# Second attention: values multiplied for two heads in one visit, turned probabilities kept in eight tiles

## The reference

```python
q = (rmsnorm_2(q_lat, q_norm_g[l]) @ w_uq[l]).reshape(B, S, H, QK_NOPE + QK_ROPE)
q_rope = rotary(q[..., QK_NOPE:], positions)
kv = (rmsnorm_2(kv_lat, kv_norm_g[l]) @ w_ukv[l]).reshape(B, S, H, QK_NOPE + V_HEAD)
y_mla = causal_block_attention(q, k, v)          # H = 16 heads, V_HEAD = 64, 128-query blocks
merged = (jax.nn.sigmoid(g_rnn) * (y_rnn @ w_proj_rnn[l])
          + jax.nn.sigmoid(g_mla) * (y_mla @ w_proj_mla[l]))
x = x + gate1 * (merged @ w_out[l])
```

## Time and profile before

| | us |
|---|---|
| median of three runs | 1893.08 |
| lowest and highest | 1892.84, 1893.96 |
| the profiled execution | 1891.63 |
| its span | 1889.8 |
| PE busy | 1854.6 |
| DVE, ACT, POOL busy | 1055.6, 754.4, 279.5 |

### The profile page before, as it was taken

How to read it: one execution, slowest core, us unless ns; L and a number is a source line. 1 busy time by engine, 2 the same in 40 slices (tenths; PEclk the granted TensorE clock), 3 DMA queues, 4 the chain that set the end, 5 groups by cost and what they waited for, 6 DMA issues and landing times.

```text
span 1889.8 us, 21234 instructions
## 1 busy us (share of the span) xinstructions
PE 1854.6 (98%) x8304; PEld 1460.7 (77%) x8304; DVE 1055.6 (56%) x1569; ACT 754.4 (40%) x1192; POOL 279.5 (15%) x362
## 2 busy tenths in 40 slices
PE   9999999999999999999999999999999999999998
PEld 7788888778878888888887777766668788888886
DVE  7754553655566545553577594455535566435643
ACT  6445444443344222222444553344434344324431
POOL 4566535100000000000001040311110000000000
PEclk9999999999999999999999999999999999999999
DMA  5222223234335545552323223312114223233321
GB/s 206 90 84 84 67 84 98 62 95 145 92 125 179 180 157 188 198 174 84 129 78 108 82 67 123 101 45 78 34 44 156 79 86 94 89 101 97 93 81 65
DMA packets 64403, 199.44 MB, mean 106 GB/s; under 512 B 7152, under 2 KB 11504, under 8 KB 64304
## 3 DMA queue, kind: packets, MB, share of 16 engines
q1 hardware_dynamic: 64304, 198.09, 32.6%
HBM read 189.68 MB, written 8.39 MB: 105 GB/s over the span
## 4 chain that ended last, share of the span: by engine, by line
PE 70%; issue 20%; DVE 6%; ACT 3%; DMA 0%; POOL 0%; POOLq 0%; SPq 0%; DVEq 0%; ACTq 0%
PE bank L251 20%; PE bank L253 19%; PE bank L252 19%; PE bank L636 2%; PE bank L665 2%; PE bank L651 1%; PE bank L544 1%; DVE wlo L1365 1%; DVE tile L1895 1%; ACT whi L811 1%; PE bank L297 1%; PE bank L356 1%; PE bank L340 1%; PE bank L386 0%; DVE tile L1987 0%
## 5 line engine op out<-in xcount | busy, mean ns | idle before, releaser
L251 PE MATMUL bank<-tiler,whi 128*128 128x512 f32 x2272 | 920.9, 405 | 10.6 <-DVE tiler L1392 4.2
L253 PE MATMUL bank<-tiler,wlo 128*128 128x512 f32 x2272 | 899.0, 396 | 0.0
L252 PE MATMUL bank<-tiler,whi 128*128 128x512 f32 x2272 | 898.9, 396 | 0.0
L811 ACT ACTIVATE whi<-raw 128x1024 fp32r<-128x1024 f32 x285 | 300.1, 1055 | 626.1 <-PE bank L253 619.5
L251 PEld LDWEIGHTS bank<-tiler,whi 128*128 128x128 f32 x2272 | 430.0, 189 | 130.2 <-issue 25.6
L253 PEld LDWEIGHTS bank<-tiler,wlo 128*128 128x128 f32 x2272 | 429.7, 189 | 101.1
L252 PEld LDWEIGHTS bank<-tiler,whi 128*128 128x128 f32 x2272 | 430.4, 189 | 95.0 <-issue 3.1
L1365 DVE TENSOR_TENSOR wlo<-raw,whi 128x1024 fp32r<-128x1024 f32 x262 | 324.9, 1244 | 294.0 <-ACT whi L811 293.8
L2140 POOL TENSOR_TENSOR stat<-stat,scl 128x4 f32<-128x4 f32 x7 | 7.1, 1016 | 1135.3 <-DVE stat L1383 702.6
L2131 POOL TENSOR_TENSOR wlo<-raw,whi 128x1024 fp32r<-128x1024 f32 x23 | 54.5, 2370 | 241.3 <-ACT whi L811 241.3
L2079 DVE SCALAR_TENSOR_TENSOR tile<-bank,sm,tile 128x511 f32<-128x511 f32 x44 | 33.0, 750 | 96.9 <-ACT tile L1339 61.9
(11 more groups left out here) (362 smaller groups left out, 1632.0 us busy)
## 6 DMA issues: line engine op xcount, KB each, us to landing
raw<-wst SPq DMA_DIRECT2D x285, 512.0 KB, 3.6
wide<-wadaT SPq DMA_DIRECT2D x48, 512.0 KB, 3.5
tile<-xT SPq DMA_DIRECT2D x16, 256.0 KB, 6.0
spare<-tile SPq DMA_DIRECT2D x16, 256.0 KB, 2.0
tile<-spare SPq DMA_DIRECT2D x16, 256.0 KB, 5.2
out<-tile SPq DMA_DIRECT2D x8, 256.0 KB, 2.0
tile<-gblk SPq DMA_DIRECT2D x5, 256.0 KB, 4.8
us<-tile SPq DMA_DIRECT2D x4, 256.0 KB, 2.0
```

What stands on the lines that cost most here:

```text
L251: e.matmul(bank, whi[:, o:o + 128], hi, start=start, stop=False)
L252: e.matmul(bank, whi[:, o:o + 128], lo, start=False, stop=False)
L253: e.matmul(bank, wlo[:, o:o + 128], hi, start=False, stop=stop).then_inc(*sig("blk", n))
L811: e.activation(whi[:, c % NHL * W:(c % NHL + 1) * W], raw[:, c % NRAW * W:(c % NRAW + 1) * W], ACT.Copy).then_inc(*sig("hi", c))
```

## The change

`mtimes` is now called in odd heads only and takes both heads of the pair: for each key block first head h-1 (lower half of `B[7]`, left half of the array), then head h (upper half, right half of the array). Each turned block of two heads now has a tile of its own, so `PTM` has eight tiles, and its copies wait for the `mtimes` of two heads back, or, in head 1, for the parking of the tile. The wait for the copy-out of the pair before stands at `mtimes(h, 0)` of odd heads. To make room, `GR2` gets other tiles, and its loads are all issued behind the weight chunks up to that of `pm` 2: five after the last block of `in2`, three after the last scores.

```diff
-QM, KM, PM, PTM, RM = (70, 71), (75, 78), 34, (39, 40, 41), (79, 74)
-GR2 = [24, 25, 26, 27, 28, 29, 70, 71]
+QM, KM, PM, PTM, RM = (70, 71), (75, 78), 34, ((24, 25, 26, 27), (28, 29, 39, 40)), (79, 74)
+GR2 = [66, 65, 64, 63, 62, 70, 71, 75]
...
             def mtimes(h, kb):
-                rows_ = slice(64 * (h % 2), 64 * (h % 2) + 64)
                 c0 = kb * 128
                 e.wait_ge(*at("mptv" if kb == 1 else "mpt", 4 * h + kb))
-                if kb == 0 and h % 2 == 0 and h:
+                if kb == 0 and h > 1:
                     e.wait_ge(*at("oplo", "ym", h // 2 - 1))
-                if h == 0 and kb == 0:
+                if h == 1 and kb == 0:
                     e.wait_ge(*at("pr_ev", 7))
...
-                vo = h % 8 * 64
-                e.matmul(B[7][rows_, c0:512], F(VS[h // 8][kb])[:, vo:vo + 64], F(PTM[(4 * h + kb) % 3])[:, c0:512],
-                         start=kb == 0, stop=True, skip_group_check=True).then_inc(*sig("mpv", h, kb))
+                for x in (h - 1, h):
+                    rows_ = slice(64 * (x % 2), 64 * (x % 2) + 64)
+                    vo = x % 8 * 64
+                    e.matmul(B[7][rows_, c0:512], F(VS[x // 8][kb])[:, vo:vo + 64], F(PTM[x % 2][kb])[:, c0:512],
+                             start=kb == 0, stop=True, skip_group_check=True).then_inc(*sig("mpv", x, kb))
...
                     work(1)
-                    mtimes(h, 0)
+                    if h % 2:
+                        mtimes(h, 0)
                     mscore(h + 1, 1)
                     work(2)
                     mscore(h + 1, 0)
                     work(3)
                     mturn(h, 2)
-                    mtimes(h, 1)
+                    if h % 2:
+                        mtimes(h, 1)
                     work(4)
                     work(5)
                     mturn(h, 3)
                     work(6)
-                    mtimes(h, 2)
-                    mtimes(h, 3)
+                    if h % 2:
+                        mtimes(h, 2)
+                        mtimes(h, 3)
                     work(7)
...
-                if p >= 3:
-                    e.wait_ge(*at("mpv", (p - 3) // 4, (p - 3) % 4))
-                if p == 0:
-                    e.wait_ge(*at("sp5", 0))
-                if p == 2:
-                    e.wait_ge(*at("sp7", 0))
-                e.activation(F(PTM[p % 3])[:, c0:512], B[5 + kb % 2][:, c0:512], ACT.Copy).then_inc(*sig("mpt", p))
+                if h >= 2:
+                    e.wait_ge(*at("mpv", h - 2, kb))
+                if h == 1 and kb >= 2:
+                    e.wait_ge(*at("sp%d" % (kb + 3), 0))
+                e.activation(F(PTM[h % 2][kb])[:, c0:512], B[5 + kb % 2][:, c0:512], ACT.Copy).then_inc(*sig("mpt", p))
...
-            until("uq", 8)
-            for m in range(6):
+            until("pm", 2)
+            e.wait_ge(*made("in2", 31))
+            for m in range(5):
                 e.wait_ge(*at("sp%d" % m, 0))
                 e.dma_start(F(GR2[m]), spare2[m]).then_inc(*sig("sp%d" % m, 1, by=16))
-            until("pm", 2)
             e.wait_ge(*at("msc", 15, 0))
-            for m in range(6, 8):
+            for m in range(5, 8):
```

More of the change, by code:

```diff
@@ L2006, in pt_copy @@
                 e.wait_ge(*at("mtr", h, 1))
[L2007 to L2011, removed]
+                if h >= 2:
+                    e.wait_ge(*at("mpv", h - 2, 1))
+                e.tensor_copy(F(PTM[h % 2][1])[:, 128:512], B[6][:, 128:512]).then_inc(*sig("mptv", p))
             def ym_lo(j):
```

## The result

| | before | after |
|---|---|---|
| median of four runs, us | 1892.96 | 1907.51 |
| lowest and highest | 1891.67, 1893.96 | 1906.10, 1910.75 |
| profiled execution | 1891.63 | 1906.85 |
| its span | 1889.8 | 1905.1 |
| mean granted clock of PE | 0.993 | 0.987 |

The changed kernel is slower: 1.008 of before, 95% interval 1.0062 to 1.0097, so 14.5 us. The forecast was 1891.5 with a range up to 1902.5. None of the forecast's cases is what happened: the halves of the array overlap fully, which is better than forecast, and more than the whole gain is lost elsewhere.

The account below looks back on a forecast made before the run. TensorE time was taken to bound the second attention, with a chain through VectorE's normalisation setting the end of even heads. Even heads -9.3 and odd heads +7.7 gave -1.6 us, from 1893.08 to 1891.5; range 1884 to 1902.5.

Parts of the forecast that it names:

- the forecast's cases: Second attention, chances: three passes for four 0.50, no overlap 0.27, full overlap 0.15, clock 0.05, no chain 0.03.
- Price of a visit, 3.09 us in an even head: Even heads, TensorE: dropping the visits of block 0 (1.10), block 1 (0.99), blocks 2 and 3 (1.00) removes 3.09 us.
- Only a part of it shows, since the chain holds even heads: Even heads: query copy, rotation, normalisation set the end; heads 2 to 12 gain 0.80 each, head 0 1.42, head 14 3.09.
- The second head adds 0.96 us to an odd head: Odd heads' visits: a pair takes three passes for four, adding 0.43, 0.32 and 0.21 us; +7.7 over 8 heads; chance 0.50.
- the other head's first pass is behind it in the queue: Odd heads' visits: head A's pass 2 runs with head B's pass 1, nothing else, so three passes for four.
- Nothing on GpSimd: Second attention: the prediction has no word on POOL (GpSimd) and no term for it in its sum.
- Nothing there changes, so the next head starts 0.80 earlier: Even heads, VectorE from rotation to normalisation: durations stay as before, so the 0.80 us from the earlier query copy carries through.
- the rival that the new idle costs clock: Some 1.9 us of TensorE idle, seven times, each followed by 3.4 us at half clock: +10, 1903; chance 0.05.
- the idle is broken in two: Ahead of odd heads' first turn: the next head's first projection step breaks the new idle of some 1.9 us in two.
- Places, parked tiles, queue of SP at 0: Eight places for turned blocks, later loads of parked tiles and 16 loads in a row on SP: taken to cost 0.
- outside 13.2 to 13.7: Sign, second attention: the forecast is wrong if odd heads don't lie at 13.2 to 13.7 us.
- a clock below 1.00: Sign, second attention: the forecast is wrong if the clock falls below 1.00 between 1215 and 1417 us.

## Why the prediction was wrong

- **Price of a visit, 3.09 us in an even head**: right. Head 14, which has no chain, fell by 3.10.
- **Only a part of it shows, since the chain holds even heads**: right in kind and nearly in size. Where the collision is taken away, heads 2 to 12 fell by 0.98 each for 0.80, head 0 by 1.59 for 1.42, in sum 10.6 for 9.3. The query copy moved up by 0.98 within the head: 0.51 from the score for 0.45, and ACT starts an instruction 0.1 us before the last one's end, which I had not counted.
- **The second head adds 0.96 us to an odd head**: wrong, it adds 0.01 to 0.02 (12.48 for 12.46). The step that failed is "the other head's first pass is behind it in the queue". It rested on rows of one half only, and those can't tell whether the other half would have waited. After, the first passes of the two heads' 512-column matmuls start 0.007 us apart (1288.724 and 1288.731). The size is -7.6 us against the sum. With the 1.3 of the point above it is the whole distance from 1891.5 to the 1882.6 of the run with GpSimd's wait, so that the range, from 1884 on, would have been missed at its lower end without the collision.
- **Nothing on GpSimd**: this is the step that decided the case. The prediction says "Nothing there changes, so the next head starts 0.80 earlier" of DVE's stretch from query copy to normalisation, and of POOL no word, although the change pulled forward the PE work that releases ACT's rounding and so POOL's subtraction, and pulled the normalisation forward by less. In the trace of before the subtraction followed the normalisation with half a microsecond to spare. The normalisation took 2.05 us for 0.29, seven times: 12.1 us.
- **Idle and clock**: the rival that the new idle costs clock had been given 0.05 and 1903. It came true through the longer idle, for 12.8 us. It was named, its price (1.7 us each time) was right in six of seven heads (3.1 in head 7), and its chance was too small: one idle of 1.88 us, behind one of 0.39, was enough in six of seven heads (the run with four filling matmuls). In the run with GpSimd's wait the idles were 0.39 and 1.00 and the clock stayed up. Whether that is because the idle is broken in two, as the prediction had it, or because it is shorter in all, isn't shown.
- **Places, parked tiles, queue of SP at 0**: right, 1893.15 against 1893.14.

Together: 1891.5 - 1.3 - 7.6 + 12.1 + 12.8 = 1907.5. Two of the signs that the prediction named for its being wrong came: odd heads at 14.1 and, without collision and clock, at 12.5, outside 13.2 to 13.7, and a clock below 1.00.

## What to carry to other kernels

Before a change pulls work forward, list for each engine what is released by it, GpSimd's instructions too, and lay them over what VectorE does then: a short VectorE instruction on a critical chain that starts just behind a long GpSimd one can cost the rest of the latter, and a wait on the idle engine was the cure here. Two float32 matmuls of 64 columns that write different halves of the partitions cost as much as one here, in both orders tried. And an idle of TensorE of about 2 us can have two prices, itself and the clock's fall behind it, so count the idles that a saving leaves, not only the saving.

## What the runs showed of the hardware that was not expected

- Two plain float32 matmuls in the left and right half of the array: 1.01 us for two of 512 columns, against 1.00 for one, and 1.44 for 0.80 (256 and 128 columns) when both are in one half.
- The order among them made no difference in the third visit: 0.81 with A, A, B, B, 0.80 with A, B, A, B.
- A VectorE instruction of 0.29 us took 2.05 beside GpSimd's subtraction, and one of 0.68 took 2.73; a start 0.14 us ahead of GpSimd's was enough to keep the length, and then GpSimd took 2.75 for 2.35.
- Idles of TensorE of 2.76 us in odd heads: a clock of 0.50 behind all seven; 2.1 us (the run with the copy-out moved): behind five of six; 1.88 us: behind six of seven; 1.00 and 0.54 us: behind none.
- The low clock lasts 3.4 us in most heads and 6.8 in some (one of seven after, two of five with the copy-out moved); what sets this stays open.
